# Gate/up products of the FFN in seven block products instead of eight, FFN blocks in three parts

## The chip, the cores and the metric

The kernel runs on one core of one Trainium2 chip. The metric is the device time of one execution in microseconds (us), taken as the median of several runs.

## The reference

One inference step of a two-layer hybrid decoder trunk for 512 prompt tokens and 8 sample tokens, all in float32. Each layer is `x += 0.5 * FFN_1(rms(x))`, then `x += Mixer(rms(x))`, then `x += 0.5 * FFN_2(rms(x))`; the mixer of layer 0 is a convolution module beside stick-breaking attention, that of layer 1 a Mamba-2 block. The change lies in the FFN, which runs four times:

```
def swiglu_ffn(x, norm_w, w_gate, w_up, w_down):   # 1024 -> 2816 -> 1024
    h = rmsnorm(x, norm_w)
    return (jax.nn.silu(h @ w_gate) * (h @ w_up)) @ w_down
```

## The kernel before

The activations lie transposed in SBUF: `xT` has the 1024 features as 8 blocks (KB) of 128 partitions and the NT = 520 tokens as columns, in two halves of H2 = 260. Every product is made of three matmuls: both operands are split into a high part, rounded to fp32r (`hh`, `wh`, `hid_h`), and the remainder (`hl`, `wl`, `hid_l`), and high x high, high x low and low x high are accumulated (`mm3`). The RMS factor `rstd` is multiplied in after the product.

The four FFN stages are `stage_ffn(0)` to `stage_ffn(3)`; the attention mixer (`stage_a`) follows stage 0, stages 1 and 2 follow one another, and the Mamba mixer (`stage_m`) lies ahead of stage 3. A stage is a row of slots, each with up to 2048 weight columns per partition. A gate/up slot ("f") takes one of the NF = 22 blocks of 128 hidden features: 8 x 128 columns of the gate matrix and 8 x 128 of the up matrix, 96 matmuls of 128 x 128 by 260 columns. A down slot ("d") takes one of the 8 output blocks for the hidden blocks of a part. FPARTS cuts the 22 hidden blocks in two parts of 12 and 10: 12 f slots, 8 d slots, 10 f slots, 8 d slots. Loops (`Fori`) take two slots a turn, u = 0 and u = 1; the first two of a stage are written out.

Each weight slot n passes through buffers of two entries, p = n % 2:
- SyncE (SP) loads `raw[p]` in two transfers, once `wl` of slot n - 2 is made (semaphore `w_ready`).
- ScalarE (ACT) makes `wh[p]` from it (`split_hi`, L212), once TensorE has ended slot n - 2 (`w_used`).
- VectorE (DVE) makes `wl[p] = raw[p] - wh[p]` (`split_lo`, L216) and raises `w_ready`, on which TensorE (PE) waits ahead of the slot.

PSUM is used in two halves of four banks, b = 4 * p. After an f slot, in the order of each engine's program: DVE multiplies gate (`gact`, L678) and up (`hidf`, L680) by `rstd` out of PSUM; ACT takes silu (L530); DVE multiplies the two (L684); ACT rounds `hid_h` (L532); DVE makes `hid_l` (L687) and raises `slot_out`. DVE and ACT prepare slot n + 1 ahead of this work of slot n. After a d slot DVE adds half the product to `xT` (L691). In the last part of the stages 0 to 2 ACT and DVE then make the next stage's `hh` (L277) and `hl` (L281), and in the last part of every stage GpSimd (POOL) sums the squares (L272, L274) for the next norm. At a stage's start PE forms the mean (`norm_mean`), ACT the root (`norm_root`, `sdev`), and DVE its reciprocal (`norm_rstd`, `rstd`), which slot 0 waits for ahead of its evacuation; PE's slot 1 waits for `sdev`, as the mean lies in its banks. In stage 0 POOL adds the squares during slot 0 (L356).

## Time and profile before

| | |
|---|---|
| median of 3 runs | 2532.5 us (2532.11 to 2532.87) |
| profiled execution | 2535.86 us, its span 2534.1 us |
| mean granted TensorE clock | 0.963 of full speed |
| TensorE matmul | 2364.5 us busy, 93% of the span, 19297 instructions |
| VectorE, ScalarE, GpSimd | 1316.2 us (52%), 782.6 us (31%), 475.4 us (19%) |
| matmuls of line L239 (all projections) | 68% of the chain that ended last |
| DMA | 248.19 MB, mean 98 GB/s |

The profile is of one execution, on the only core used. Busy times of engines overlap, so their shares don't add up to the span; the chain that ended last is followed back from the last instruction and does. The granted clock of TensorE has two levels, shown as 1.00 (2.4 GHz) and 0.50 (1.2 GHz); values between are means over a stretch.

### The profile page before, as it was taken

The numbers are of one execution on the slowest core, as the hardware profiler recorded it, in microseconds if no ns is written. First come the engines' busy times: TensorE is split into PE (matmuls) and PEld (weight loads), VectorE is DVE, ScalarE is ACT, GpSimd is POOL, SyncE is SP. The second block draws the span as 40 slices with busy tenths as digits, with TensorE's granted clock in tenths as the row PEclk, the third lists the DMA queues.
The fourth block names the chain that finished last, engine by engine and source line by source line (L and its number), as shares of the span: only waits on it lengthen the run. The fifth ranks groups of instructions, "written<-read, shape, count | busy, mean of one in ns | idle before, by whom it ended". The sixth has DMA issues, their size and how long they took to land.

```text
span 2534.1 us, 45882 instructions
## 1 busy us (share of the span) xinstructions
PE 2364.5 (93%) x19297; PEld 2262.5 (89%) x19297; DVE 1316.2 (52%) x1393; ACT 782.6 (31%) x917; POOL 475.4 (19%) x353
## 2 busy tenths in 40 slices
PE   6999999986889999999999999989898978999998
PEld 6999999873559999999999999979797857999998
DVE  4443445767664443345443345777777757443442
ACT  4221222215442222223222223443433323221223
POOL 2000002683213000003000003051525264000002
PEclk9999999986898999999999999999999998999999
DMA  4323325562522333324323323333333322323322
GB/s 120 98 81 104 83 78 171 150 199 68 167 84 67 83 85 97 95 69 118 85 80 103 89 75 105 87 106 99 96 109 92 96 84 78 95 75 108 88 75 76
DMA packets 411834, 248.19 MB, mean 98 GB/s; under 512 B 11634, under 2 KB 386778, under 8 KB 411664
## 3 DMA queue, kind: packets, MB, share of 16 engines
q1 hardware_dynamic: 411255, 246.28, 34.1%
q8 instruction: 89, 1.46, 0.3%
q14 instruction: 30, 0.25, 0.0%
q10 hardware_dynamic: 460, 0.20, 0.0%
HBM read 232.48 MB, written 14.61 MB: 98 GB/s over the span
## 4 chain that ended last, share of the span: by engine, by line
PE 77%; DVE 10%; ACT 5%; POOL 4%; issue 3%; DMA 1%; SPq 0%; ACTq 0%; POOLq 0%; DVEq 0%
PE PS L239 68%; POOL prod L910 2%; PE PS L1128 2%; DVE xcs L2113 1%; PE PS L1074 1%; DVE wl L216 1%; ACT wh L212 1%; DVE cbuf L1309 1%; PE PS L1918 1%; PE PS L1007 1%; PE PS L1018 1%; DVE xcs L2295 1%; DVE hl L281 1%; DVE grs L2197 1%; PE PS L1822 1%
## 5 line engine op out<-in xcount | busy, mean ns | idle before, releaser
L239 PE MATMUL PS<-hh,wh 128*128 128x260 f32 x3792 | 774.9, 286 | 26.0 <-DVE hl L281 12.9
L239 PE MATMUL PS<-hh,wl 128*128 128x260 f32 x3792 | 768.4, 284 | 0.0
L239 PE MATMUL PS<-hl,wh 128*128 128x260 f32 x3792 | 768.0, 284 | 0.0
L239 PEld LDWEIGHTS PS<-hh,wh 128*128 128x128 f32 x3792 | 589.5, 190 | 37.8 <-issue 30.6
L239 PEld LDWEIGHTS PS<-hh,wl 128*128 128x128 f32 x3792 | 588.8, 190 | 0.2
L239 PEld LDWEIGHTS PS<-hl,wh 128*128 128x128 f32 x3792 | 588.2, 190 | 0.2
L216 DVE TENSOR_TENSOR wl<-raw,wh 128x2048 fp32r<-128x2048 f32 (+2 forms) x195 | 449.3, 2304 | 217.1 <-ACT wh L212 217.0
L212 ACT ACTIVATE wh<-raw 128x2048 fp32r<-128x2048 f32 (+2 forms) x195 | 354.7, 1819 | 300.2 <-PE PS L239 266.0
L272 POOL TENSOR_TENSOR sqr<-xT 128x520 f32 (+1 forms) x47 | 51.6, 1098 | 1498.8 <-DVE xT L691 1417.5
L239 PE MATMUL PS<-hid_l,wh 128*128 128x260 f32 x1408 | 283.6, 283 | 0.0
L239 PE MATMUL PS<-hid_h,wl 128*128 128x260 f32 x1408 | 283.3, 282 | 0.0
L239 PE MATMUL PS<-hid_h,wh 128*128 128x260 f32 x1408 | 283.2, 282 | 0.0
L678 DVE TENSOR_TENSOR gact<-PS,rstd 128x520 f32<-128x520 f32 x88 | 61.6, 700 | 387.9 <-PE PS L239 387.9
L530 ACT ACTIVATE gact<-gact 128x520 f32<-128x520 f32 x88 | 56.2, 638 | 656.3 <-DVE gact L678 656.3
L239 PEld LDWEIGHTS PS<-hid_h,wh 128*128 128x128 f32 x1408 | 217.0, 188 | 0.0
L239 PEld LDWEIGHTS PS<-hid_h,wl 128*128 128x128 f32 x1408 | 216.7, 188 | 0.0
L239 PEld LDWEIGHTS PS<-hid_l,wh 128*128 128x128 f32 x1408 | 216.6, 188 | 0.0
L691 DVE SCALAR_TENSOR_TENSOR xT<-PS,xT 128x520 f32 (+1 forms) x64 | 44.8, 700 | 209.2 <-PE PS L239 209.2
L1696 POOL TENSOR_TENSOR ms_t<-xdt,bcs 128x512 f32<-128x512 f32 x32 | 48.1, 1502 | 310.7 <-DMA bcs<-brow 277.4
L687 DVE TENSOR_TENSOR hid_l<-hidf,hid_h 128x520 f32 (+1 forms) x88 | 61.7, 701 | 80.2 <-ACT hid_h L532 80.2
L1309 DVE SCALAR_TENSOR_TENSOR cbuf<-uA,cwv,cbuf 128x512 f32<-128x512 f32 x90 | 83.3, 926 | 2.7
L532 ACT ACTIVATE hid_h<-hidf 128x520 f32 (+1 forms) x88 | 56.3, 639 | 81.5 <-DVE hidf L684 81.5
(304 smaller groups left out, 2439.8 us busy)
## 6 DMA issues: line engine op xcount, KB each, us to landing
raw<-in_ffn_gate_dram SPq DMA_DIRECT2D x88, 512.0 KB, 3.9
raw<-in_ffn_up_dram SPq DMA_DIRECT2D x88, 512.0 KB, 5.2
raw<-in_ffn_down_dram SPq DMA_DIRECT2D x64, 384.0 KB, 4.1
raw<-in_ffn_down_dram SPq DMA_DIRECT2D x64, 320.0 KB, 3.6
raw<-in_m_in_proj_dram SPq DMA_DIRECT2D x40, 512.0 KB, 5.3
page<-in_cache_sb_v_dram SPq DMA_DIRECT2D x48, 256.0 KB, 3.0
raw<-in_ab_in_proj_dram SPq DMA_DIRECT2D x20, 512.0 KB, 5.6
ms_b<-in_state_ssm_dram SPq DMA_DIRECT2D x32, 256.0 KB, 3.0
```

The costliest lines, as they stand in the source:

```text
L212: act.activation(wh[:, p, 0:cols], raw[:, p, 0:cols], ACT.Copy).then_inc(w_hi, 1)
L216: dve.tensor_tensor(wl[:, p, 0:cols], raw[:, p, 0:cols], wh[:, p, 0:cols].bitcast(F32), ALU.subtract).then_inc(w_ready, 1)
L239: ins = pe.matmul(out, x[:, k0, c:c + m], y[:, k, half * H2:(half + 1) * H2], start=k == 0 and a == 0, stop=k == nk - 1 and a == 2)
L272: pool.tensor_tensor(sqr[:, :], xT[:, j, :], xT[:, j, :], ALU.mult).then_inc(norm_sq, 1)
L530: act.activation(gact[:, u, :], gact[:, u, :], ACT.Silu).then_inc(silu_done, 1)
L532: act.activation(hid_h[:, u + 2 * t, :], hidf[:, u, :], ACT.Copy)\
L678: dve.tensor_tensor(halves(gact[:, u, :]), PS[:, b:b + 2, 0:H2], r, ALU.mult)\
L687: dve.tensor_tensor(hid_l[:, u + 2 * t, :], hidf[:, u, :], hid_h[:, u + 2 * t, :].bitcast(F32), ALU.subtract).then_inc(slot_out, 1)
L910: pool.tensor_tensor(prod[:, i % 2, :], kplace[(b % 2) * NPG + pg], qb[:, b % 2, :], ALU.mult)\
L1128: ins = pe.matmul(PS[:, 2 * j + h, 0:H2], x[:, n % 2, (j * KB + k) * P:(j * KB + k + 1) * P], y[:, k, h * H2:(h + 1) * H2], start=first an ...
L1309: ch(dve.scalar_tensor_tensor(out=out, in0=uA[:, c, w:w + T], scalar=col, in1=out, op0=ALU.mult, op1=ALU.add))
L1696: pool.tensor_tensor(t, col(xdt, b), bc, ALU.mult).then_inc(S["g_chain"], 1)
```

## The change

The 22 hidden blocks are cut in three parts of 8, 8 and 6, so a stage has 24 d slots instead of 16. In each part every second f slot, u = 1, except the first such slot (t = 0), is computed as a 2x2 block product in seven products: the rows of the 2x2 weight matrix are gate and up, the columns are the two halves of the 1024 input features (KH = 4 blocks each), and the 2x2 token matrix has the halves of the features and the halves of the tokens. A seven-product slot has 7 x 4 x 3 = 84 matmuls of 260 columns, an ordinary one 96.

The scheme needs sums of the operands. Token sums T1 to T4 are made once a stage during its first two slots (`token_sums` on ACT and DVE, behind the split of the next slot and ahead of the evacuation); weight sums S1, S2, S4 and the one written over A21 for each seven-product slot, on DVE, in two pieces inside the evacuation of the slot two back (`weight_sums`). ACT then rounds 2048 + 1536 columns (`seven_hi`) and DVE subtracts as many (`seven_lo`). The products are combined out of PSUM by `seven_first` (behind q6), `seven_second` (behind q7 and q4) and `seven_third` (behind q3), with q1 copied by ACT. The waits for earlier stores at the start of the stages 1 and 3 move ahead of the token sums, the semaphores of the set-up and of the end are merged (renamed `turn_...`), the buffers of the set-up are freed ahead of stage 0, the first two f slots of each part and the last two slots of each phase on ACT and DVE are written out, and the split ahead of a d slot covers only that slot's columns instead of 2048 for every second one.

```diff
-    FA = (NF // 2 + 1) // 2 * 2
-    FPARTS = [(0, FA), (FA, NF - FA)]
+    FA = (NF + 5) // 6 * 2
+    FPARTS = [(0, FA), (FA, FA), (2 * FA, NF - 2 * FA)]
+    LAST = len(FPARTS) - 1
...
+        NZ = [n // 2 - 1 for _, n in FPARTS]
+        KH = KB // 2
+        A11, A12, A21, A22 = (slice(i * KH * P, (i + 1) * KH * P) for i in range(4))
+        S1, S2, S4 = (slice(i * KH * P, (i + 1) * KH * P) for i in range(3))
...
+                wsum = sb_in(st, f"wsum{f}", [P, 3 * KH * P])
+                wsh = sb_in(st, f"wsh{f}", [P, 3 * KH * P], F32R)
+                wsl = sb_in(st, f"wsl{f}", [P, 3 * KH * P], F32R)
+                gst = sb_in(st, f"gst{f}", [P, 6, H2])
+                nrstd = sb_in(st, f"nrstd{f}", [P, NT])
+                with ExitStack() as tst:
+                    tch = sb_in(tst, f"tch{f}", [P, 4, KH, H2], F32R)
+                    tcl = sb_in(tst, f"tcl{f}", [P, 4, KH, H2], F32R)
...
+                def seven(kind, t, u):
+                    return kind == "f" and u == 1 and not (isinstance(t, int) and t == 0)
...
+                def zn(part, t):
+                    return f * sum(NZ) + sum(NZ[:part]) - 1 + t
...
+                            if seven(kind, t, u):
+                                act.wait_ge(q_mm, 4 * zn(part, t) + 1)
+                                act.activation(gst[:, 5, :], PS[:, 4 * (n % 2), 0:H2], ACT.Copy).then_inc(t_act, 1)
+                            if u == 0 and seven(kind, t, 1):
+                                seven_hi(n + 1 + 2 * t, (n + 1) % 2, (n + 1) // 2 + t, zn(part, t))
+                            elif not is_last(kind, part, t, u):
+                                split_hi(act, n + 1 + 2 * t, (n + 1) % 2, (n + 1) // 2 + t, ahead(kind, part, t, u, n))
+                            if s0 == 0 and isinstance(t, int) and t == 0:
+                                token_sums(u)
+                            if is_first(s0, t, u):
...
+                        def seven_hi(m, p, half, z):
+                            act.wait_ge(landed[p], 32 * half + 32)
+                            act.wait_ge(w_used, m + 1)
+                            act.wait_ge(t_dve, TW + 4 * z + 4)
+                            act.activation(wh[:, p, :], raw[:, p, :], ACT.Copy)
+                            act.activation(wsh[:, :], wsum[:, :], ACT.Copy).then_inc(w_hi, 1)
+                        def token_sums(u):
+                            ks = range(u * KH // 2, (u + 1) * KH // 2)
+                            if u == 0:
+                                earlier_done(act)
+                            for k in ks:
+                                if u == 1 and k % 2 == 1:
+                                    act.wait_ge(slot_out, S0 + 3)
+                                act.activation(xw[k % 2][:, 0:2, :], halves(xT[:, k, :]), ACT.Copy,
+                                               scale=vec[:, fw + k:fw + k + 1])
+                                act.activation(xw[k % 2][:, 2:4, :], halves(xT[:, KH + k, :]), ACT.Copy,
+                                               scale=vec[:, fw + KH + k:fw + KH + k + 1]).then_inc(t_act, 1)
+                            for k in ks:
+                                act.wait_ge(t_dve, TD + tcount(k, 3))
+                                act.activation(tch[:, :, k, :], tf[k % 2], ACT.Copy).then_inc(t_act, 1)
+                            if u == 1:
+                                act.wait_ge(norm_rs, ni + 1)
+                                act.activation(nrstd[:, :], rstd[:, :], ACT.Copy, scale=-1.0).then_inc(t_act, 1)
...
+                                    if q == 1 and u == 0 and not (isinstance(t, int) and t == 0):
+                                        pe.wait_ge(q_out, 4 * zn(part, t) + 1)
...
+                        def seven_products(p, z, prev):
+                            y, x = 4 * p, 4 - 4 * p
+                            w = lambda sl: (wh[:, p, sl], wl[:, p, sl])
+                            ws = lambda sl: (wsh[:, sl], wsl[:, sl])
+                            b = lambda k0, half: tuple(a[:, k0:k0 + KH, half * H2:(half + 1) * H2] for a in (hh, hl))
+                            tc = lambda i: (tch[:, i, :, :], tcl[:, i, :, :])
+                            pe.wait_ge(t_dve, TD + 4 * KH)
+                            for name, bank, (ah, al), (bh, bl) in (
+                                    ("q1", y, w(A11), b(0, 0)), ("q5", y + 2, ws(S1), tc(T1)),
+                                    ("q2", x + 2, w(A12), b(KH, 0)), ("q6", x + 3, ws(S2), tc(T2)),
+                                    ("q7", y + 3, w(A21), tc(T3)), ("q4", y + 1, w(A22), tc(T4)),
+                                    ("q3", y, ws(S4), b(KH, 1))):
+                                if name == "q2":
+                                    pe.wait_ge(up_scaled, prev)
+                                if name == "q3":
+                                    pe.wait_ge(t_act, TZ + z + 1)
+                                for k in range(KH):
+                                    c = slice(k * P, (k + 1) * P)
+                                    for i, (l, r) in enumerate(((ah, bh), (ah, bl), (al, bh))):
+                                        ins = pe.matmul(PS[:, bank, 0:H2], l[:, c], r[:, k, :],
+                                                        start=k == 0 and i == 0, stop=k == KH - 1 and i == 2)
+                                if name in ("q1", "q6", "q7", "q4"):
+                                    ins.then_inc(q_mm, 1)
+                            return ins
...
+                        def seven_lo(m, p):
+                            dve.wait_ge(w_hi, m + 1)
+                            dve.tensor_tensor(wl[:, p, :], raw[:, p, :], wh[:, p, :].bitcast(F32), ALU.subtract)
+                            dve.tensor_tensor(wsl[:, :], wsum[:, :], wsh[:, :].bitcast(F32), ALU.subtract)\
+                                .then_inc(w_ready, 1)
+                        def token_sums(u):
+                            ks = range(u * KH // 2, (u + 1) * KH // 2)
+                            if u == 0:
+                                earlier_done(dve)
+                            for k in ks:
+                                x4, t4 = xw[k % 2], tf[k % 2]
+                                dve.wait_ge(t_act, TA + (KH * u) + k % 2 + 1)
+                                dve.tensor_tensor(t4[:, T1:T3 + 1, :], x4[:, 0:4:3, :],
+                                                  x4[:, 1:2, :].to_broadcast([P, 2, H2]), ALU.subtract).then_inc(t_dve, 1)
+                                dve.wait_ge(t_dve, TD + tcount(k, 1))
+                                dve.scalar_tensor_tensor(out=t4[:, T2, :], in0=t4[:, T3, :], scalar=-1.0, in1=x4[:, 0, :],
+                                                         op0=ALU.mult, op1=ALU.subtract).then_inc(t_dve, 1)
+                                dve.wait_ge(t_dve, TD + tcount(k, 2))
+                                dve.scalar_tensor_tensor(out=t4[:, T4, :], in0=t4[:, T2, :], scalar=-1.0, in1=x4[:, 2, :],
+                                                         op0=ALU.mult, op1=ALU.subtract).then_inc(t_dve, 1)
+                            for k in ks:
+                                dve.wait_ge(t_act, TA + (KH * u) + KH // 2 + k % 2 + 1)
+                                dve.tensor_tensor(tcl[:, :, k, :], tf[k % 2], tch[:, :, k, :].bitcast(F32),
+                                                  ALU.subtract).then_inc(t_dve, 1)
+                        def weight_sums(i, m, p, half, z):
+                            if i == 0:
+                                dve.wait_ge(landed[p], 32 * half + 32)
+                                dve.wait_ge(t_dve, TW + 4 * z)
+                                dve.tensor_tensor(wsum[:, S1], raw[:, p, A21], raw[:, p, A22], ALU.add)\
+                                    .then_inc(t_dve, 1)
+                                dve.wait_ge(t_dve, TW + 4 * z + 1)
+                                dve.tensor_tensor(raw[:, p, A21], raw[:, p, A21], raw[:, p, A11], ALU.add)\
+                                    .then_inc(t_dve, 1)
+                            else:
+                                dve.wait_ge(t_dve, TW + 4 * z + 1)
+                                dve.tensor_tensor(wsum[:, S2], wsum[:, S1], raw[:, p, A11], ALU.add)\
+                                    .then_inc(t_dve, 1)
+                                dve.wait_ge(t_dve, TW + 4 * z + 3)
+                                dve.tensor_tensor(wsum[:, S4], wsum[:, S2], raw[:, p, A12], ALU.add)\
+                                    .then_inc(t_dve, 1)
+                        def seven_first(x, z):
+                            dve.wait_ge(q_mm, 4 * z + 2)
+                            dve.wait_ge(t_act, TZ + z + 1)
+                            dve.tensor_tensor(gst[:, 0:3:2, :], gst[:, 5:6, :].to_broadcast([P, 2, H2]),
+                                              PS[:, x + 2:x + 4, 0:H2], ALU.add).then_inc(q_out, 1)
+                        def seven_second(y, z):
+                            dve.wait_ge(q_mm, 4 * z + 3)
+                            dve.wait_ge(q_out, 4 * z + 5)
+                            dve.tensor_tensor(gst[:, 3:5, :], gst[:, 2:3, :].to_broadcast([P, 2, H2]),
+                                              PS[:, y + 2:y + 4, 0:H2], ALU.add).then_inc(q_out, 1)
+                            dve.wait_ge(q_mm, 4 * z + 4)
+                            dve.wait_ge(q_out, 4 * z + 6)
+                            dve.tensor_tensor(halves(hidf[:, 1, :]), gst[:, 4:5, :].to_broadcast([P, 2, H2]),
+                                              PS[:, y + 1:y + 3, 0:H2], ALU.add).then_inc(q_out, 1)
+                        def seven_third(y, z):
+                            dve.tensor_tensor(gst[:, 1, :], gst[:, 3, :], PS[:, y, 0:H2], ALU.add).then_inc(q_out, 1)
+                            dve.wait_ge(q_out, 4 * z + 8)
...
                         def slot(t, u):
                             n = N0 + s0 + u
-                            if not is_last(kind, part, t, u):
-                                split_lo(dve, n + 1 + 2 * t, (n + 1) % 2, ahead(kind, part, u))
-                            if n == N0 and isinstance(t, int):
+                            z = zn(part, t) if kind == "f" else None
+                            is7 = seven(kind, t, u)
+                            b = 4 * (n % 2)
+                            if is7:
+                                seven_first(4 - b, z)
+                            if u == 0 and seven(kind, t, 1):
+                                seven_lo(n + 1 + 2 * t, (n + 1) % 2)
+                            elif not is_last(kind, part, t, u):
+                                split_lo(dve, n + 1 + 2 * t, (n + 1) % 2, ahead(kind, part, t, u, n))
+                            if s0 == 0 and isinstance(t, int) and t == 0:
+                                token_sums(u)
+                            if is_first(s0, t, u):
                                 norm_rstd(dve, ni)
-                            b = 4 * (n % 2)
+                            if is7:
+                                seven_second(b, z)
                             dve.wait_ge(w_used, n + 3 + 2 * t)
-                            if n == N0 and isinstance(t, int) and f == 1:
-                                dve.wait_ge(stored, 32)
-                                dve.wait_ge(SA["kv_out"], 80)
-                            if n == N0 and isinstance(t, int) and f == 3:
-                                dve.wait_ge(stored, 16 * stores_before)
-                                dve.wait_ge(SM["ho_st"], 16 * MG)
-                                for i in range(4):
-                                    dve.wait_ge(SM[f"ms_st{i}"], 16 * MG * B // 4)
                             if kind == "f":
                                 i = H0 + f0 + u + 1 + 2 * t
                                 r = halves(rstd[:, :])
-                                dve.tensor_tensor(halves(gact[:, u, :]), PS[:, b:b + 2, 0:H2], r, ALU.mult)\
+                                gate, up, ur = PS[:, b:b + 2, 0:H2], PS[:, b + 2:b + 4, 0:H2], r
+                                if is7:
+                                    seven_third(b, z)
+                                    dve.wait_ge(t_act, TA + 2 * KH + 1)
+                                    gate, up, ur = gst[:, 0:2, :], halves(hidf[:, u, :]), halves(nrstd[:, :])
+                                more = u == 1 and not (isinstance(t, int) and t == iters - 1)
+                                dve.tensor_tensor(halves(gact[:, u, :]), gate, r, ALU.mult)\
                                     .then_inc(g_scaled, 1)
-                                dve.tensor_tensor(halves(hidf[:, u, :]), PS[:, b + 2:b + 4, 0:H2], r, ALU.mult)\
+                                dve.tensor_tensor(halves(hidf[:, u, :]), up, ur, ALU.mult)\
                                     .then_inc(up_scaled, 1)
+                                if more:
+                                    weight_sums(0, n + 2 + 2 * t, n % 2, (n + 2) // 2 + t, z + 1)
                                 dve.wait_ge(up_scaled, i)
                                 dve.wait_ge(silu_done, i)
                                 dve.tensor_tensor(hidf[:, u, :], hidf[:, u, :], gact[:, u, :], ALU.mult)\
                                     .then_inc(hid_done, 1)
+                                if more:
+                                    weight_sums(1, n + 2 + 2 * t, n % 2, (n + 2) // 2 + t, z + 1)
...
```

## Rows read from the trace of the kernel before

**Rows 1.** The page: busy us (share) xinstructions, and the chain's shares.
```profile
PE 2364.5 (93%) x19297; PEld 2262.5 (89%) x19297; DVE 1316.2 (52%) x1393; ACT 782.6 (31%) x917; POOL 475.4 (19%) x353
...
PE 77%; DVE 10%; ACT 5%; POOL 4%; issue 3%; DMA 1%; SPq 0%; ACTq 0%; POOLq 0%; DVEq 0%
```

**Rows 2.** The chain in order of time, stage 0: start us, us, what.
```profile
45.40 374.75 PE PS L239 x3120
```

**Rows 3.** Busy by stretch: length, PE, PEld, DVE, ACT, POOL, granted clock, DMA, GB/s.
```profile
45.40:56.93 11.53, 11.53 (x96) 11.53 (x97) 8.38 (x6) 4.33 (x4) 0.00 (x0) 1.00 0.01 1
68.75:80.28 11.53, 11.53 (x98) 11.53 (x97) 5.00 (x5) 3.08 (x3) 0.00 (x0) 1.00 0.34 91
```

**Rows 4.** Timeline of DVE, gate/up slots of stage 0: start us, us, instruction.
```profile
57.21 0.70 DVE L678 TENSOR_TENSOR gact<-PS,rstd 128x520 f32<-128x520 f32 x1 [1.42 <-PE PS L239]
...
68.75 0.70 DVE L678 TENSOR_TENSOR gact<-PS,rstd 128x520 f32<-128x520 f32 x1 [4.55 <-PE PS L239]
69.36 0.69 DVE L680 TENSOR_TENSOR hidf<-PS,rstd 128x520 f32<-128x520 f32 x1
...
71.85 0.70 DVE L687 TENSOR_TENSOR hid_l<-hidf,hid_h 128x520 f32 x1 [0.93 <-ACT hid_h L532]
73.53 2.29 DVE L216 TENSOR_TENSOR wl<-raw,wh 128x2048 fp32r<-128x2048 f32 x1 [0.99 <-ACT wh L212]
```

**Rows 5.** Timeline of ACT, the same slot.
```profile
69.48 0.64 ACT L530 ACTIVATE gact<-gact 128x520 f32<-128x520 f32 x1 [7.61 <-DVE gact L678]
...
71.60 1.90 ACT L212 ACTIVATE wh<-raw 128x2048 fp32r<-128x2048 f32 x1
```

**Rows 6.** Starts of stages 0 and 2: timelines of DVE, ACT; POOL's line L356.
```profile
35.82 2.29 DVE L216 TENSOR_TENSOR wl<-raw,wh 128x2048 fp32r<-128x2048 f32 x1 [5.21 <-ACT wh L212]
...
1196.48 2.42 DVE L216 TENSOR_TENSOR wl<-raw,wh 128x2048 fp32r<-128x2048 f32 x1 [0.91 <-ACT wh L212]
1200.20 3.40 DVE L299 RECIPROCAL rstd<-sdev 128x520 f32<-128x520 f32 x1 [1.30 <-ACT sdev L295]
...
44.65 0.69 ACT L295 ACTIVATE sdev<-PS,epst 128x520 f32<-128x520 f32 x1 [7.56 <-PE PS L289]
...
1199.47 0.70 ACT L295 ACTIVATE sdev<-PS,epst 128x520 f32<-128x520 f32 x1 [1.72 <-PE PS L289]
...
L356 POOL TENSOR_TENSOR ssum<-ssum,xin x8: 1291/1306/3273, 30.5 to 42.1; 128x520 f32<-128x520 f32 x8
```

**Rows 7.** Timelines in the down slots of stage 0's last part: DVE, ACT, POOL.
```profile
361.03 1.49 DVE L216 TENSOR_TENSOR wl<-raw,wh 128x1280 fp32r<-128x1280 f32 x1 [0.33 <-ACT wh L212]
...
400.18 0.70 DVE L691 SCALAR_TENSOR_TENSOR xT<-PS,xT 128x520 f32 x1 [1.28 <-PE PS L239]
402.01 0.76 DVE L281 SCALAR_TENSOR_TENSOR hl<-xT,vec,hh  x1 [1.14 <-ACT hh L277]
403.04 2.25 DVE L216 TENSOR_TENSOR wl<-raw,wh 128x1280 fp32r<-128x1280 f32 x1 [0.27 <-ACT wh L212]
...
401.75 1.26 ACT L212 ACTIVATE wh<-raw 128x1280 fp32r<-128x1280 f32 x1
...
402.27 1.67 POOL L274 TENSOR_TENSOR ssum<-ssum,sqr 128x520 f32<-128x520 f32 x1
```

**Rows 8.** Timeline of PE in the Mamba stage, one bank twice.
```profile
1671.53 0.39 PE L1788 MATMUL PS<-rowsR,sel 128*128 128x512 f32 x1
1671.76 0.40 PE L1790 MATMUL PS<-maskR,identR 128*128 128x512 f32 x1
```

**Rows 9.** Busy time by stretch at a long wait, and PE's timeline at a short one.
```profile
1581.90:1585.40 3.50, 0.15 (x3) 0.05 (x1) 3.47 (x3) 0.81 (x3) 0.00 (x0) 0.72 1.11 304
1585.50:1590.20 4.70, 4.70 (x22) 4.70 (x23) 2.78 (x3) 2.35 (x3) 3.70 (x4) 0.50 0.61 152
...
45.40 0.51 PE L239 MATMUL PS<-hh,wh 128*128 128x260 f32 x2 [0.79 <-ACT sdev L295]
```

**Rows 10.** DMA issues: destination, queue, count, KB each, median us to landing.
```profile
raw<-in_ffn_up_dram SPq DMA_DIRECT2D x88, 512.0 KB, 5.2
```

More of the change, by code:

```diff
@@ L432, in stage_ffn @@
                 hidf = sb_in(st, f"hidf{f}", [P, 2, NT])
+                wsum = sb_in(st, f"wsum{f}", [P, 3 * KH * P])
[6 more added lines that the diff above has]
+                    tcl = sb_in(tst, f"tcl{f}", [P, 4, KH, H2], F32R)
+                T1, T3, T2, T4 = range(4)
+                fw = V_NORM[FFN_W[f]]
+                xw = [halves2(gact), halves2(hidf)]
+                tf = [gst[:, 0:4, :], wsum[:, 0:4 * H2].rearrange("p (i c) -> p i c", i=4)]
+                TA, TD = f * (2 * KH + 1 + sum(NZ)), f * (4 * KH + 4 * sum(NZ))
+                TZ, TW = (f + 1) * (2 * KH + 1), (f + 1) * 4 * KH
                 H0 = f * NF
@@ L453, in stage_ffn, with run @@
                 mean_out = 4 * ((N0 + NS_FFN - 2) % 2)
-                def run(eng, phase, slot):
+                def run(eng, phase, slot, peel=False):
                     kind, part, s0, iters = phase
@@ L461, in run @@
                         return
[L462 removed]
+                    head = int(kind == "f")
+                    tail = int(peel)
                     if head:
@@ L465, in run, with is_first, ahead, tcount @@
                         slot(0, 1)
[L466 removed]
+                    with eng.Fori(head, iters - tail) as t:
                         slot(t, 0)
                         slot(t, 1)
+                    if tail:
+                        slot(iters - 1, 0)
+                        slot(iters - 1, 1)
                 def is_end(kind, part):
[L471 to L475 removed]
+                    return f == 3 and kind == "d" and part == LAST
+                def seven(kind, t, u):
+                    return kind == "f" and u == 1 and not (isinstance(t, int) and t == 0)
+                def is_first(s0, t, u):
+                    return s0 == 0 and u == 0 and isinstance(t, int) and t == 0
+                def zn(part, t):
+                    return f * sum(NZ) + sum(NZ[:part]) - 1 + t
+                def ahead(kind, part, t, u, n):
+                    if isinstance(t, int):
+                        return slot_cols(n + 1 + 2 * t)
+                    return 2048 if kind == "f" else FPARTS[part][1] * P
+                def tcount(k, i):
+                    return 8 * (k // 2) + (3 * (k % 2) + i if i <= 3 else 6 + k % 2 + 1)
+                def earlier_done(eng):
+                    if f == 1:
+                        eng.wait_ge(stored, 32)
+                        eng.wait_ge(SA["kv_out"], 80)
+                    if f == 3:
+                        eng.wait_ge(stored, 16 * stores_before)
+                        eng.wait_ge(SM["ho_st"], 16 * MG)
+                        for i in range(4):
+                            eng.wait_ge(SM[f"ms_st{i}"], 16 * MG * B // 4)
                 def is_last(kind, part, t, u):
@@ L533, in slot @@
                                     .then_inc(hid_hi, 1)
-                            elif part == 1 and next_col is not None:
+                            elif part == LAST and next_col is not None:
                                 act.wait_ge(slot_out, S0 + s0 + u + 3 + 2 * t)
@@ L694, in slot @@
                                     .then_inc(slot_out, 1)
-                                if part == 1 and next_col is not None:
+                                if part == LAST and next_col is not None:
                                     norm_split_lo(dve, ni + 1, next_col, u + 2 * t)
-                        run(dve, phase, slot)
+                        run(dve, phase, slot, peel=True)
                     if f == 3:
```

118 lines of the change are left out of this document (60 added, 58 removed).

## The prediction

> **What bounds the kernel now.** I read the shares and the chain that ended last first [rows 1]: TensorE (PE) is busy 93% of the span and makes 77% of the chain. The chain in order of time [rows 2] shows what that means in a feed-forward (FFN) stage: from the second slot of stage 0 to the stage's end stands one piece, 3120 matmuls in 374.75 us without a wait, 0.1201 us each. In a gate/up slot, 96 matmuls, PE is busy for all 11.53 us at clock 1.00, while VectorE (DVE) works 5.00 and ScalarE (ACT) 3.08 us [rows 3]. So what is taken from PE comes back one for one as long as nothing becomes later than PE. What can become late is the weight preparation of the slot after next: it overwrites this slot's wh, so it can't begin before PE has ended the slot. Call that moment T. DVE's gact starts at T + 0.28 (slot 1 starts at 45.40 and takes 11.53, gact starts at 57.21 [rows 3, 4]). From there the timelines of DVE and ACT [rows 4, 5] are to be read as one chain: hidf, silu, product, hid_h, then wh at gact + 2.85, and wl, which ends at gact + 7.07, that is T + 7.35. PE needs it at T + 11.53. The slack is 4.2 us a slot, and the change must live on it.
>
> **Scale of costs.** DVE takes 0.70 us for 520 columns, 1.49 for 1280, 2.29 for 2048 [rows 4, 7]: 0.16 us + 1.04 ns a column. So 260, 512, 768, 1024, 1536 columns are estimated at 0.43, 0.69, 0.96, 1.22, 1.76. ACT takes 0.64, 1.26, 1.90 [rows 5, 7]: 0.21 us + 0.825 ns a column; 768, 1024, 1040, 1536 are 0.84, 1.05, 1.07, 1.48. An instruction that need not wait starts 0.08 before the end of the one ahead (gact to hidf [rows 4]); for one that waits for the one ahead I take 0.05 after it.
>
> **A. Products.** Parts of 8, 8 and 6 blocks have 3, 3 and 2 seven-product slots: 8 a stage, 32 in all. Each issues 84 matmuls for 96: 32 x 12 x 0.1201 = -46.1 us. The products run one after the other into one bank, where now two banks alternate. The nearest row is the pair L1788, L1790, 512 columns into one bank, 0.23 apart [rows 8]: 0.45 ns a column against 0.46. I take no difference; for the other bound I add 10 ns to each of 2688 matmuls, +27.
>
> **B. Weight sums.** From T, the end of one seven-product slot, to the next one's weights: the third combination starts at 0.28, gact 0.76, hidf 1.38, S1 1.99, the sum into A21 2.73, the product 3.34, S2 3.96, S4 4.70 (ends 5.39). ACT: wh from 5.46, wsh from 7.28 to 8.76. DVE: wl from 8.79, wsl from 11.00 to 12.76; PE 0.06 later, 12.82. The slot between is an ordinary one and ends at 11.53: PE waits 1.29, and of the 1.44 saved 0.15 is left. For the first seven-product slot of a part the slot two back is ordinary and has no third combination: 12.34, a wait of 0.81. Five a stage are of the first kind, two of the second (part 0's is in C): 20 x 1.29 + 8 x 0.81 = +32.3. Inside the slot nothing is late: up_scaled comes 1.2 after its start, q2 wants it after 2.9; the split of the next slot ends 1.1 before PE. Bounds: three waits in the chain may cost 0.1 more each, 28 x 0.3 = +8; at the other end the chain ends early enough and B is 0 (rival 1). I stay with the sum, whose links are all rows.
>
> **C. Token sums at the start of a stage.** Per k, DVE makes three sums (1.58 with waits), ACT copies 1040 columns, DVE subtracts 1040 (1.24). Two k come in slot 0, two in slot 1, each behind split_lo and ahead of gact. In slot 1 that is 2 x 1.58 + 2.4 = 5.5 us ahead of the chain of B. Stage 2 as the example: DVE is free at 1198.9, its sums and ACT's copy end at 1203.1, ACT loads the root's table (1.3) and sdev starts at 1204.4 instead of 1199.47 [rows 6]: PE waits 0.3. rstd takes 3.40, gact of slot 0 moves by 3.2, split_lo of slot 2 ends at 1215.5, the token work at 1221.0, and w_ready of the first seven-product slot is 12.0 later, 1233.0. Slot 2 ends at 1228.2: PE waits 4.8. The same count gives 3.1 in stage 1 and 3.9 in stage 3. In stage 0 POOL still adds squares until 43.4; one of its eight adds took 3.27 us instead of 1.31 while DVE's wl of 35.82 ran at its usual 2.29 [rows 6]. So the two take turns: DVE's six sums last from 38.1 to about 46, sdev comes near 49 instead of 44.65, and PE waits 3.9 more there and 2.5 at the first seven-product slot. Waits: 0.3 + 4.8 + 3.1 + 3.9 + 3.9 + 2.5 = 18.5. Five of them are near 2.5 us or over. After some 3.4 us of almost no matmuls at 1582 the granted clock, 0.72 over that stretch, was 0.50 for the next 4.7 us, with 22 matmul starts where 39 fit [rows 9]: 2 us lost. The 0.79 us wait at 45.40 [rows 9] was followed by a slot at 1.00 [rows 3]. Five times 2: C = +28.5. Bounds: 10 (half hidden, clock kept) and 40 (every start like stage 0).
>
> **D. Entry to a down phase.** Down slots have 8, 8, 6 blocks instead of 12 and 10: 5.77 and 4.32 us; there are 32 more of them but no more matmuls. The part's last hidden tile is ready at T + 4.4 (third combination 0.48, then 3.80 from gact to the end of hid_l [rows 4]). PE gets to it after 7 x 6 matmuls, 5.04, but in the last part after 5 x 6, 3.60: 0.8 x 4. The second down slot's weights come at T + 5.90 against 5.77, and 5.42 against 5.12: 0.13 x 8 + 0.3 x 4. D = +5.4. Transfers shrink with the slots, and a slot's pair of 512 KB now lands some 6 us after DVE lets it go [rows 10]: hidden. Bounds 0 and 8.
>
> **E. Pace of the last part.** DVE evacuates xT, ACT makes hh, DVE hl, ACT wh, DVE wl; POOL squares and adds beside them. With 1280 columns wl takes 2.25 us there and 1.49 where POOL is idle; POOL's add runs until 403.94 [rows 7]. With 768 columns wl could start at xT + 2.5, waits for POOL until xT + 3.6 and ends at xT + 4.55. xT starts at T + 0.33, so w_ready is T + 4.9 against a slot of 4.32: 0.6 x 6 slots x 3 stages = +10.8. In stage 3 transposes lengthen the slot by half a microsecond: 0. Were the turns with POOL absent, wl would end at xT + 3.5 and E be 0; that and 16 are the bounds.
> The Trainium skill (GPSIMD Engine Reference, section Key points) says that GpSimd shares its SBUF interfaces with VectorE and contends with VectorE instructions that have two SBUF inputs. By that rule wl waits too, and the rows agree; without it the sum would be 24, not 35.
>
> **F. Into the next stage.** The last down slot has 4.32 us to hide the split of 2048 columns: wh starts at T + 1.90, wl ends at T + 6.26 (2.42 long, as at 1196.48 [rows 6]): PE waits 2.0 after stages 0 and 1; after stage 2 comes a slot of 256 columns. F = +4.0.
>
> **Sum.** -46.1 + 32.3 + 28.5 + 5.4 + 10.8 + 4.0 = +34.9. The profiled execution took 2535.9 (span 2534.1), 3.4 over the median; on it the sum is 2570.8, on the median of 2532.5 it is 2567.
>
> **Rivals.** (1) The preparation hides: B to F at nothing, 2486. For it: DVE is busy 43% and ACT 27% of a slot [rows 3]. Against: the chain of B is latency, each link waits for the last. It decides once B is under 0.3 a slot and C to F together under 30. 8%. (2) C hides, the rest as summed: 2532.5 + 6.4 = 2539. Against: the order split_lo, token_sums, gact. 10%. (3) B hides, C to F as summed: 2532.5 + 2.6 = 2535. 8%. (4) Each of B's 28 waits also halves the clock, at 1.7 us lost: +48, 2615. Against: 0.79 us of idle did not do it; between 0.79 and 3.4 these rows leave it open. 6%. My own case has 68%, from 2550 to 2592.
> The Trainium skill (TensorE: Matmul & The Clock Gate, section "A second HAM failure mode: psum-queue depth-cycling") tells of small idles between matmul groups that made the clock swing again and again. That is rival 4; the rows so far have no wait of 1.3 us in an FFN stage to judge it by.
>
> **Chances.** 0.2%, 5 us, is about what a measurement here tells from no change. Faster is rival 1, 0.08; same is rival 3, 0.08; slower the rest, 0.84. The range reaches from rival 2 to the upper end of my case: 2539 to 2592.
>
> **What would show it.** Right: 384 fewer matmuls; PE waiting for DVE's wsl before each seven-product slot, 1.3 us, 0.8 in the first of a part, 3 to 5 in the first of a stage with the clock at 0.50 behind it; PE waiting some 0.6 for wl in the last down phases. Wrong: no wait behind wsl (A alone is left), matmuls over 0.121 apart in the seven products, or the clock at 0.50 at steady pace.

## The result and the profile after

The changed kernel takes 2564.4 us (median of 4 runs, 2561.07 to 2568.44), the kernel before 2532.3 in the same comparison: ratio 1.013, 95% interval 1.0113 to 1.0148, +32.1 us. The forecast was 2567. The profiled execution is the quickest of the four, 2561.07 us with a span of 2559.4, 25.3 over the span of before.

The page of the changed kernel, with the rows that answer to [rows 1]:

```profile
PE 2336.7 (91%) x18913; PEld 2224.5 (87%) x18913; DVE 1586.0 (62%) x1809; ACT 865.5 (34%) x1065; POOL 476.0 (19%) x353
...
PE 55%; DVE 23%; ACT 9%; issue 7%; POOL 4%; DMA 1%; SPq 0%; ACTq 0%; DVEq 0%; POOLq 0%
```

There are 384 matmuls fewer, as counted. PE's part of the chain that ended last falls from 77% to 55%, and DVE's rises from 10% to 23%: the FFN stages are no longer one piece of matmuls. Who waited for whom, PE alone, stage 0 (us in total, times, longest):

```profile
PE PS L733 <- DVE wsl L789: 9.2, 8, 1.9
PE PS L239 <- ACT sdev L299: 3.5, 1, 3.5
PE PS L239 <- issue: 1.4, 1, 1.4
PE PS L239 <- DVE wl L216: 0.8, 3, 0.3
PE PS L239 <- DVE hid_l L894: 0.5, 1, 0.5
```

L733 is the seven-product slot, and all 8 of the stage wait for `wsl`, the low part of the weight sums. The row `issue` is the first matmul of the next stage (F): it starts 0.10 us behind the end of DVE's `wl`. The same row is 20.6 us in 16 waits up to 1220 us and, for the other two stages:

```profile
PE PS L733 <- DVE wsl L789: 23.9, 16, 5.1
```

PE's timeline shows the sizes: the late `sdev` of stage 0, the first three seven-product slots of that stage, and the first one of stages 1, 2 and 3 (start, us, instruction, idle before):

```profile
48.46 0.80 PE L239 MATMUL PS<-hh,wh 128*128 128x260 f32 x2 [3.45 <-ACT sdev L299]
...
76.36 0.36 PE L733 MATMUL PS<-hh,wh 128*128 128x260 f32 x1 [1.95 <-DVE wsl L789]
99.29 0.36 PE L733 MATMUL PS<-hh,wh 128*128 128x260 f32 x1 [1.13 <-DVE wsl L789]
122.30 0.36 PE L733 MATMUL PS<-hh,wh 128*128 128x260 f32 x1 [1.21 <-DVE wsl L789]
...
852.94 0.46 PE L733 MATMUL PS<-hh,wh 128*128 128x260 f32 x1 [4.04 <-DVE wsl L789]
...
1242.68 0.56 PE L733 MATMUL PS<-hh,wh 128*128 128x260 f32 x1 [4.21 <-DVE wsl L789]
...
2195.41 0.56 PE L733 MATMUL PS<-hh,wh 128*128 128x260 f32 x1 [5.15 <-DVE wsl L789]
```

The idle time printed is 0.16 us less (0.26 at `sdev`) than what the gap between two matmul starts has over their usual distance of 0.12; below I count by the gaps, since the end of a matmul is modelled. The pair of slots from 76.36 took 22.93 and the next one 23.01, against 23.06 before: of the 1.44 us that twelve matmuls save, almost nothing is left.

Busy time by stretch, columns as in [rows 3]: a seven-product slot, and what follows two of the long waits.

```profile
76.20:86.30 10.10, 9.94 (x83) 9.97 (x84) 6.32 (x8) 3.36 (x4) 0.00 (x0) 1.00 0.38 105
48.46:55.00 6.54, 6.54 (x32) 6.54 (x33) 5.64 (x5) 2.80 (x4) 0.00 (x0) 0.55 0.00 0
852.94:856.60 3.66, 3.66 (x18) 3.66 (x19) 2.38 (x4) 2.05 (x4) 0.00 (x0) 0.53 0.68 193
```

Behind 3.45 us of idle TensorE ran at its lower clock: 32 matmuls in 6.54 us, where 54 fit, so some 2.6 us were lost. Behind 1.95 us (the slot of 76.36) and behind every wait of 1.1 to 1.3 it stayed at 1.00.

### The profile page after: what moved, and what is told of

Read it like the earlier page. It is cut to its first block, busy times and chain, and to the rows that moved or that the text cites. A ratio compares the mean times of both kernels' runs of the same rounds, so it can differ in the third digit from the quotient of the medians.

```text
span 2559.4 us, 46123 instructions
## 1 busy us (share of the span) xinstructions
PE 2336.7 (91%) x18913; PEld 2224.5 (87%) x18913; DVE 1586.0 (62%) x1809; ACT 865.5 (34%) x1065; POOL 476.0 (19%) x353
## 4 chain that ended last, share of the span: by engine, by line
PE 55%; DVE 23%; ACT 9%; issue 7%; POOL 4%; DMA 1%; SPq 0%; ACTq 0%; DVEq 0%; POOLq 0%
PE PS L239 34%; PE PS L733 12%; POOL prod L1117 2%; DVE wl L216 2%; DVE wsl L789 2%; ACT wsh L623 2%; PE PS L1335 2%; DVE wl L788 1%; ACT wh L212 1%; ACT wh L622 1%; DVE hidf L889 1%; DVE cbuf L1516 1%; DVE xcs L2320 1%; PE PS L2125 1%; DVE wsum L828 1%
## 5 line engine op out<-in xcount | busy, mean ns | idle before, releaser
L239 PE MATMUL PS<-hh,wh 128*128 128x260 f32 (+1 forms) x2768 | 568.9, 287 | 31.8 <-DVE hl L285 12.9
L239 PE MATMUL PS<-hh,wl 128*128 128x260 f32 (+1 forms) x2768 | 561.7, 285 | 0.0
L239 PE MATMUL PS<-hl,wh 128*128 128x260 f32 (+1 forms) x2768 | 561.4, 285 | 0.0
L239 PEld LDWEIGHTS PS<-hh,wh 128*128 128x128 f32 (+1 forms) x2768 | 430.9, 190 | 44.6 <-issue 32.3
L216 DVE TENSOR_TENSOR wl<-raw,wh 128x2048 fp32r<-128x2048 f32 (+3 forms) x195 | 373.3, 1914 | 136.0 <-ACT wh L212 135.7
L239 PEld LDWEIGHTS PS<-hh,wl 128*128 128x128 f32 (+1 forms) x2768 | 430.6, 190 | 0.2
L239 PEld LDWEIGHTS PS<-hl,wh 128*128 128x128 f32 (+1 forms) x2768 | 430.4, 190 | 0.2
L212 ACT ACTIVATE wh<-raw 128x2048 fp32r<-128x2048 f32 (+3 forms) x195 | 281.8, 1445 | 360.7 <-PE PS L239 324.6
L788 DVE TENSOR_TENSOR wl<-raw,wh 128x2048 fp32r<-128x2048 f32 x32 | 73.4, 2292 | 89.1 <-ACT wsh L623 89.1
L733 PE MATMUL PS<-hh,wh 128*128 128x260 f32 x256 | 76.6, 299 | 44.4 <-DVE wsl L789 44.4
```

Source lines behind the costliest of these rows:

```text
L212: act.activation(wh[:, p, 0:cols], raw[:, p, 0:cols], ACT.Copy).then_inc(w_hi, 1)
L216: dve.tensor_tensor(wl[:, p, 0:cols], raw[:, p, 0:cols], wh[:, p, 0:cols].bitcast(F32), ALU.subtract).then_inc(w_ready, 1)
L239: ins = pe.matmul(out, x[:, k0, c:c + m], y[:, k, half * H2:(half + 1) * H2], start=k == 0 and a == 0, stop=k == nk - 1 and a == 2)
L733: ins = pe.matmul(PS[:, bank, 0:H2], l[:, c], r[:, k, :], start=k == 0 and i == 0, stop=k == KH - 1 and i == 2)
L788: dve.tensor_tensor(wl[:, p, :], raw[:, p, :], wh[:, p, :].bitcast(F32), ALU.subtract)
```

## The experiments

All ratios are to the kernel before, run on the same chip beside each (medians 2531.8 for the first four, 2531.28 for e5 to e8, 2530.65 for e9). Where a run is set against the changed kernel, that is its median of 2564.4 from its own comparison, whose kernel before was 0.5 to 1.7 us slower than these. My theory: the change loses in the latency of three chains (B, C, E), each a link too long, and not in throughput or in the clock at steady pace.

**e1_parts_alone.** Three parts stay, all slots have eight products, there are no sums.

```diff
 def seven(kind, t, u):
-    return kind == "f" and u == 1 and not (isinstance(t, int) and t == 0)
+    return False
...
-    token_sums(u)
```

> Three parts of 8, 8, 6 blocks and all the rest of the edit, but every gate/up slot ordinary: no seven products, no token sums, no weight sums. Theory: only the shorter down slots cost, by the waits that the trace of the changed kernel shows in the last part and at its end (5.3 + 3.1) and some 1.5 at the entries: 10 us, 2542. Rival 'the parts are free and all of the loss is the sums': 2532. Rival 'the cut in three parts is the loss': 2560 and more.

Measured 2543.71, ratio 1.0046 (1.0033 to 1.0059). PE in stage 0:

```profile
PE PS L239 <- DVE wl L216: 1.7, 3, 0.6
PE PS L239 <- ACT sdev L299: 0.8, 1, 0.8
```

So the cut into three parts costs 11.9 us by itself (interval 8.4 to 14.9; D, E and F, forecast 20), and the seven products with their sums 20.7 net: 46.1 won and 66.8 paid.

**e3_no_weight_sums** and **e4_no_token_sums** each leave one kind of sum out, so what they compute is not the FFN.

```diff
-act.activation(wsh[:, :], wsum[:, :], ACT.Copy).then_inc(w_hi, 1)
...
-dve.tensor_tensor(wsl[:, :], wsum[:, :], wsh[:, :].bitcast(F32), ALU.subtract)
```
```diff
-if s0 == 0 and isinstance(t, int) and t == 0:
-    token_sums(u)
```

> Leaves out part of the computation: no weight sums S1, S2, S4 and A21, no wsh and wsl; the products q5, q6, q3 take slices of wh and wl in their place. PE issues the same 84 matmuls a slot, token sums stay. Theory: the chain is that of an ordinary slot plus the third combination, no PE wait behind it; the first seven-product slots lose their 2 to 5.5 us waits too and the half clock behind three of them: 2564.4 - 33.7 - 16.5 - 6.6 = 2508. Rival 'seven products are slower on PE, one bank or more waits inside the slot': above 2520 with matmuls over 0.121 us apart.

> Leaves out part of the computation: no token sums; the products take slices of hh and hl in place of the token sums. Weight sums stay. Theory: the starts of the stages are as before, the first seven-product slot waits 0.8 as the others of its kind, and no clock is lost: C is gone, 2564.4 - 27 = 2537. Rival 'token sums hide behind slot 0 and 1': 2560.

e3: 2504.53, ratio 0.9899 (0.9884 to 0.9915), 59.9 below the changed kernel; no wait for `wsl` is left, the one for `sdev` stays at 3.5. e4: 2538.84, ratio 1.0034 (1.0022 to 1.0046), 25.6 below; the wait for `sdev` is back to the 0.79 of before [rows 9], and the row for `wsl` is now

```profile
PE PS L733 <- DVE wsl L789: 6.9, 8, 1.1
```

The longest is 1.1 where it was 1.9, and the waits of the steady pairs are only some 0.1 shorter (1.18 and 1.25 by the gaps, for 1.29 and 1.38). B and C are two costs, as in the sum. The long wait at the first seven-product slot of a stage belongs to both: it goes whichever kind of sum is left out.

**e2_own_signal_for_wsh.** Here B is tested at its weakest link. In the changed kernel ACT signals once, behind both of its copies; DVE's `wl` needs the first copy alone.

```diff
-act.activation(wh[:, p, :], raw[:, p, :], ACT.Copy)
-act.activation(wsh[:, :], wsum[:, :], ACT.Copy).then_inc(w_hi, 1)
+act.activation(wh[:, p, :], raw[:, p, :], ACT.Copy).then_inc(w_hi, 1)
+act.activation(wsh[:, :], wsum[:, :], ACT.Copy).then_inc(ws_hi, 1)
...
 dve.tensor_tensor(wl[:, p, :], raw[:, p, :], wh[:, p, :].bitcast(F32), ALU.subtract)
+dve.wait_ge(ws_hi, z + 1)
 dve.tensor_tensor(wsl[:, :], wsum[:, :], wsh[:, :].bitcast(F32), ALU.subtract)
```

> The changed kernel with one wait divided: ACT signals wh by itself and wsh by a second semaphore, so DVE makes wl while ACT makes wsh. No instruction is removed. Theory (latency of the weight chain): weights are ready 1.4 us sooner, T + 11.4 against 11.53, the 28 waits of 0.8 to 1.4 us vanish (-33.7), the first seven-product slot of each stage waits 1.4 less (-5.6): 2525. Rival 'volume': DVE and ACT do as much as before, nothing changes, 2564.

First the chain of B in the changed kernel, from the end of the slot that starts at 76.36: T = 76.36 + 84 x 0.1201 = 86.45. Timeline of DVE:

```profile
86.70 0.42 DVE L851 TENSOR_TENSOR gst<-gst,PS 128x260 f32<-128x260 f32 x1
87.16 0.70 DVE L881 TENSOR_TENSOR gact<-gst,rstd 128x520 f32<-128x520 f32 x1
...
91.04 0.69 DVE L828 TENSOR_TENSOR wsum<-wsum,raw 128x512 f32<-128x512 f32 x1
91.65 0.69 DVE L894 TENSOR_TENSOR hid_l<-hidf,hid_h 128x520 f32 x1
95.09 2.29 DVE L788 TENSOR_TENSOR wl<-raw,wh 128x2048 fp32r<-128x2048 f32 x1 [2.74 <-ACT wsh L623]
97.30 1.75 DVE L789 TENSOR_TENSOR wsl<-wsum,wsh 128x1536 fp32r<-128x1536 f32 x1
```

and of ACT:

```profile
91.77 1.92 ACT L622 ACTIVATE wh<-raw 128x2048 fp32r<-128x2048 f32 x1 [0.60 <-DVE wsum L828]
93.59 1.47 ACT L623 ACTIVATE wsh<-wsum 128x1536 fp32r<-128x1536 f32 x1
```

`wh` ends at 93.69, yet `wl` starts at 95.09, when `wsh` ends: DVE idles 2.74 us on the path, 1.40 of them behind the end of `wh`. `wsl` ends at 99.05, T + 12.60, and PE starts at 99.29, T + 12.84. The same two DVE instructions in e2:

```profile
92.74 2.29 DVE L789 TENSOR_TENSOR wl<-raw,wh 128x2048 fp32r<-128x2048 f32 x1 [1.37 <-ACT wh L623]
94.95 1.75 DVE L791 TENSOR_TENSOR wsl<-wsum,wsh 128x1536 fp32r<-128x1536 f32 x1
```

The third combination is at 85.71 there, so `wsl` now ends 10.99 behind it instead of 12.35: 1.36 us saved, and PE needed 1.3. In stage 0 one wait is left:

```profile
PE PS L734 <- DVE wsl L791: 0.5, 1, 0.5
```

The kernel takes 2517.79, ratio 0.9953 (0.9938 to 0.9968): 46.6 below the changed kernel, without one instruction of work removed. I had expected 7 us more, 2525, with 1.4 less of wait at the first seven-product slot of each stage. What stays of these waits in stages 0 to 3 (by the gaps) is 0.7, 1.4, 3.0 and 4.2 instead of 2.1, 4.3, 4.6 and 5.5, and the lower clock comes only behind the last of them, for 14 matmuls; the expectation had left the clock out.

**e7_pool_sums_narrow.** To see POOL's part in C and E, its squares and adds are cut from 520 to 8 columns in the changed kernel, which leaves most of the norm's sum out.

```diff
-pool.tensor_tensor(sqr[:, :], xT[:, j, :], xT[:, j, :], ALU.mult)
+pool.tensor_tensor(sqr[:, 0:8], xT[:, j, 0:8], xT[:, j, 0:8], ALU.mult)
...
-pool.tensor_tensor(ssum[:, :], ssum[:, :], sqr[:, :], ALU.add)
+pool.tensor_tensor(ssum[:, 0:8], ssum[:, 0:8], sqr[:, 0:8], ALU.add)
...
-pool.tensor_tensor(ssum[:, :], ssum[:, :], sqs[:, k, :], ALU.add)
+pool.tensor_tensor(ssum[:, 0:8], ssum[:, 0:8], sqs[:, k, 0:8], ALU.add)
```

> The changed kernel, but POOL squares and adds only 8 of 520 columns for every norm of the FFN stages, and sums start at 64 (leaves out part of the norm; all other instructions stay). Theory (DVE and POOL take turns): wl of the last down slots takes 0.96 instead of 2.06, all waits of the last parts go (-5.3), and in stage 0 sdev no longer comes late (-2.9, -1.0 of the old wait, and some 2 of clock), of which the first seven-product slot takes back 2: about 2555. Rival 'POOL is beside the point': wl stays at 2.06, sdev at its place, 2564.

Measured 2551.08, ratio 1.0084 (1.006 to 1.0108), 13.3 below the changed kernel. DVE at the start of stage 0, changed kernel first:

```profile
37.92 1.81 DVE L800 TENSOR_TENSOR gst<-gact 128x520 f32<-128x520 f32 x1
39.76 1.42 DVE L803 SCALAR_TENSOR_TENSOR gst<-gst,gact 128x260 f32<-128x260 f32 x1
41.22 1.43 DVE L806 SCALAR_TENSOR_TENSOR gst<-gst,gact 128x260 f32<-128x260 f32 x1
42.57 1.80 DVE L800 TENSOR_TENSOR wsum<-hidf 128x520 f32<-128x520 f32 x1
44.40 0.43 DVE L803 SCALAR_TENSOR_TENSOR wsum<-wsum,hidf 128x260 f32<-128x260 f32 x1
```

and e7:

```profile
38.25 0.69 DVE L800 TENSOR_TENSOR gst<-gact 128x520 f32<-128x520 f32 x1
38.98 0.43 DVE L803 SCALAR_TENSOR_TENSOR gst<-gst,gact 128x260 f32<-128x260 f32 x1
```

While POOL adds full rows a sum of 0.43 us takes 1.42 and one of 0.69 takes 1.81; with POOL's rows short, and in the changed kernel from 44.40 on, they have their usual time. The same in the last part's down slots, the changed kernel's DVE and POOL and then e7's DVE:

```profile
390.49 0.70 DVE L898 SCALAR_TENSOR_TENSOR xT<-PS,xT 128x520 f32 x1 [0.20 <-PE PS L239]
393.04 2.06 DVE L216 TENSOR_TENSOR wl<-raw,wh 128x768 fp32r<-128x768 f32 x1
```
```profile
392.61 1.67 POOL L278 TENSOR_TENSOR ssum<-ssum,sqr 128x520 f32<-128x520 f32 x1
```
```profile
392.42 0.95 DVE L216 TENSOR_TENSOR wl<-raw,wh 128x768 fp32r<-128x768 f32 x1
```

In e7 the waits for `wl` are gone, and PE's wait for `sdev` in stage 0 is 0.79 again. But the stage's first seven-product slot now waits longer than before:

```profile
73.41 0.56 PE L733 MATMUL PS<-hh,wh 128*128 128x260 f32 x1 [4.54 <-DVE wsl L789]
```

PE arrives 5.5 us earlier, at weights that come only 2.9 us earlier. So POOL is the cause of E and of the late `sdev`, and gives away less in C than its own wait shows. The Trainium skill (GPSIMD Engine Reference, section Key points), on which E drew, says that GpSimd contends with VectorE instructions that have two SBUF inputs; the sums and the splits above are such instructions, and both places agree.

**e5, e6: what is left after e2.** e5 takes e2 and makes the parts 8, 6 and 8 blocks, so that the part in which POOL works has the longer slots. e6 adds an ordinary slot in place of the first seven-product slot of each stage, 28 seven-product slots in all.

```diff
-FPARTS = [(0, FA), (FA, FA), (2 * FA, NF - 2 * FA)]
+FPARTS = [(0, 8), (8, 6), (14, 8)]
```
```diff
+def begin(part):
+    return 2 if part == 0 else 1
...
-    return kind == "f" and u == 1 and not (isinstance(t, int) and t == 0)
+    return kind == "f" and u == 1 and not (isinstance(t, int) and t < begin(part))
```

> The kernel with the own signal for wsh, and the parts ordered 8, 6, 8 instead of 8, 8, 6, so that the last part, with the norm's work beside it, has slots of 5.77 us. Theory: w_ready at T + 4.9 is in time there, so the waits of the last parts (5.3 in all) and most of those at the next stage (3.1 to 1.0) go: 2517.8 - 7.4 = 2510. Rival 'the last part is paced by something of the slot's own, as POOL': no change, 2518.

> As the run with own signal and parts 8, 6, 8, and the first seven-product slot of each stage is made ordinary, so the weight sums of the first one begin two slots later, clear of the token sums. Costs 4 x 1.44 = 5.8 of products; takes away the waits of 0.7, 1.4, 3.0 and some 3.5 us there and the half clock behind two of them, some 4. Theory: 2510 + 5.8 - 8.6 - 4 = 2503. Rival 'the token work only moves its wait to the next slot': 2510 to 2516.

e5: 2511.98, ratio 0.9925 (0.9907 to 0.9944), 5.8 below e2, with intervals that still touch; the trace decides: no wait for `wl` is left in the last part of stage 0, and E is gone. e6: 2503.3, ratio 0.9888 (0.9869 to 0.9908); 12 matmuls more in each stage, and 8.7 us faster. PE's waits of e6 in stage 0:

```profile
PE PS L239 <- ACT sdev L299: 3.5, 1, 3.5
PE PS L239 <- DVE hid_l L900: 0.5, 1, 0.5
PE PS L239 <- issue: 0.3, 1, 0.3
```

**e8, e9: where the token sums stand.** e8 moves the second half of them to the third slot in each stage; e9 besides moves those of stage 0 out of its first slot, away from POOL.

```diff
-if s0 == 0 and isinstance(t, int) and t == 0:
-    token_sums(u)
+if s0 == 0 and isinstance(t, int) and t <= 1 and u == 0:
+    token_sums(t)
```
```diff
+TOKEN_SLOTS = [(0, 1), (1, 0)] if f == 0 else [(0, 0), (1, 0)]
```

> As the run with the first seven-product slot later, and the second half of the token sums moves from slot 1 to slot 2, so that no slot carries it together with the late rstd of slot 0. Theory: what wait the token sums still cause at slot 3 (estimated 0 to 1 us a stage) goes: 1 to 3 us under that run. Rival: no difference, as it was hidden already.

> As the run with token sums in slots 0 and 2, but in stage 0 they are made in slots 1 and 2, when POOL has ended its eight adds of squares. Theory: the wait for sdev at slot 1 of stage 0 falls back from 3.7 to the 1.05 us it has without token sums, and the half clock behind it goes (some 2.6): 2504.4 - 5.3 = 2499, with the clock of that slot at 1.00. Rival 'the token sums wait the same time elsewhere': PE waits at slot 3 of stage 0 instead, 2504.

e8: 2504.38, ratio 0.9891 (0.9872 to 0.991), no difference from e6, where 1 to 3 us were expected: the rival held. With the first seven-product slot gone nothing waits for the second half of these sums any more. e9: 2500.23, ratio 0.9878 (0.9858 to 0.9898). Its start of stage 0, PE's timeline and the first slot's stretch:

```profile
45.35 0.51 PE L239 MATMUL PS<-hh,wh 128*128 128x260 f32 x2 [0.79 <-ACT sdev L299]
```
```profile
45.40:56.90 11.50, 11.50 (x96) 11.50 (x97) 9.41 (x9) 6.76 (x8) 0.00 (x0) 1.00 0.01 1
```

The long wait is gone and the first slot runs at clock 1.00. e9 has the lowest median: 30.4 us below the kernel before and 64 below the changed one. By the medians e6, e8 and e9 can't be told apart, as their intervals overlap; that the wait and the lower clock of stage 0 went is what the trace shows. Of the 28 x 12 x 0.1201 = 40.4 us of matmuls that e9 leaves out, 10 are not seen in the medians. In its profiled execution the four stages are 32.5 us shorter than in that of before, so 8 of them went inside the stages; the waits of stage 0 beyond that for `sdev` (1.2 us as printed, 2.1 by the gaps) are some 8 for four stages.

## Why the prediction was right

By the matmul starts of the profiled executions, summed over the four stages, the changed kernel's terms are as below. Measured is what a stretch takes beyond its matmuls at 0.1201 us each (for C, what it takes beyond the same stretch of before, with the matmuls left out counted back in). So each wait counts with the matmul behind it, which comes 0.07 to 0.10 late itself.

| term | forecast | measured |
|---|---|---|
| A products | -46.1 | -46.1 |
| B weight sums | +32.3 | +34.5 |
| C starts of the stages | +28.5 | +24.6 |
| D entry to down phases | +5.4 | +5.0 |
| E pace of the last part | +10.8 | +7.4 |
| F into the next stage | +4.0 | +3.3 |
| not assigned | | +1.1 |
| sum | +34.9 | +29.8 |

The sum is what the four stages took more: 10.7, 7.0, 6.8 and 5.5 us (from the first matmul of each to the first behind it). The profiled spans differ by 25.3 only, since the attention stage was 7.4 us shorter and the Mamba stage 2.8 longer, though not a line of the two was changed. The attention stage before, then after, columns as in [rows 3]:

```profile
414.24:807.82 393.58, 325.55 (x2807) 267.29 (x2805) 247.03 (x279) 135.79 (x151) 160.76 (x118) 0.88 0.46 135
```
```profile
424.78:811.00 386.22, 320.31 (x2804) 263.71 (x2805) 247.74 (x279) 135.76 (x151) 160.47 (x118) 0.89 0.47 137
```

The attention stage took 385.8 to 389.1 in e2 to e9 and 392.2 in e1, whose profiled execution was 6.4 above its median. Whether the change shortens it or single executions differ by this is open. The medians give +32.1. That the forecast of 2567 came within 3 us of 2564.4 is in part luck: C and E were 3.9 and 3.4 too high, and the stages 5.1 in all.

**A** held: 384 fewer, and the matmuls of the seven products, twelve in a row into one bank, came 0.12 apart (83 in 9.94 us in the stretch from 76.20), so the upper bound of +27 was empty. One reading ahead of the sum was off: of the 3120 matmuls of [rows 2] the last 48 belong to the next stage, which changes no term.

**B** held in place and size: waits of 1.29 to 1.41 in a steady pair for the 1.29 of the forecast, 0.79 to 0.87 for 0.81 in the first of a part, 33.6 in all. Two of its steps were off and cancelled. `wsl` ended at T + 12.60 instead of 12.76, and PE started 0.24 behind it, not 0.06. e3 shows that the weight sums cause the waits, e2 which link of the chain: ACT's second copy ahead of `wl`. The forecast's chain had that link in plain view (wl from 8.79, behind wsh's end at 8.76) and took it as given.

**C** held in place, and was 3.9 too high. At `sdev` in stage 0 PE waited 2.9 more (forecast 3.9), at the first seven-product slots 2.1, 4.3, 4.6 and 5.5 (2.5, 3.1, 4.8 with 0.3 ahead, 3.9). These 19.4 are more than the 18.5 of the forecast. The lower clock behind them cost 7.5 instead of 10: 26, 15, 12 and 26 matmuls came some 0.215 apart instead of 0.12. The first seven-product slot of stage 0, counted among the five, kept the full clock behind 1.95 us. And on balance 2.3 came back in the first slots of the stages, for the stretches at the lower clock there were shorter than before (12 matmuls for 26 in stage 1); the forecast has nothing on these. e4 takes off 25.6; it leaves a wait of 0.7 at the first seven-product slot, as at the first of any part there.

**D** held: the first down slot of the last part waited 0.69 four times for 0.8, though the hidden tile's own links add up to T + 4.56 and not 4.4 (it ended at T + 4.30). The second slot's weights were late in the last part alone, by 0.16. D has no experiment of its own. e1 holds D, E and F together at 11.9, where these terms make 15.7. It has no third combination, so its wait at that down slot is 0.27, while its waits for `wl` in stage 0 are longer (1.7 us as printed against 0.8).

**E** is the step that was furthest off, in its size. The weights came as forecast, `wl` ending 4.61 behind the evacuation for 4.55. But I priced each slot's wait against a slot without waits. The chain spans two slots: what PE waits in one slot is time that the next slot's weights already have. The waits alternate, 0.44 and 0.19, so that a pair shares the 0.6:

```profile
395.23 0.38 PE L239 MATMUL PS<-hid_h,wh 128*128 128x260 f32 x1 [0.28 <-DVE wl L216]
399.85 0.38 PE L239 MATMUL PS<-hid_h,wh 128*128 128x260 f32 x1
```

That halves the waits, to 5.3; the matmuls behind them, 0.10 late each, make it 7.4. e7 shows the cause (no wait for `wl` without POOL's rows), e5 that longer slots hide it.

**F** was a wait of 1.55 and 1.59 after stages 0 and 1 for 2.0 each.

**The rivals.** Rival 1, all preparation hides, falls by 28 waits of the steady kind. Rival 2, C hides: e4 is what it would be like, 2538.84 for its 2539 (as close by luck, since E was 3.4 too high in it), and the changed kernel is 25.6 slower. Rival 3, B hides: nearest is e2, 2517.79, where part of C went too; the changed kernel shows B in full. Rival 4, B's waits halve the clock, falls: 1.00 in the slots behind waits of 1.1 to 1.95 us, 0.53 to 0.55 behind 3.45 and 4.04. The lower clock came only behind the few long waits, so the swing of which the Trainium skill tells (TensorE: Matmul & The Clock Gate, section "A second HAM failure mode: psum-queue depth-cycling") isn't seen here, although PE idled shortly at every second slot.

## What to carry to other kernels

Work taken off the busiest engine pays only until the preparation of its operands is as long: here 4.2 us of slack a slot held all the new sums but 1.3 us, and that 1.3 ate the gain. Ask of each new link in such a chain whether its consumer needs it or merely shares its signal; a second semaphore turned +1.3% into -0.5% here, and longer slots beside POOL's work and an ordinary slot more at each stage's start made it -1.1%; with the token sums out of POOL's way it is -1.2%, a step that the trace of stage 0 shows but the medians can't. Where a chain spans two slots, price the pair and not each slot: a wait in one is cover for the next.
